# Turning attention weights with the transpose instruction in one decoder step on Trainium2

## What is computed

```
s = q @ k.T * SCALE - slope * dist            # masked
p = softmax(s)
o = p @ v
o = gate[0] * o_cmp + gate[1] * o_sel + gate[2] * o_win
h = x + concat(o, pooled) @ w_out
h = h + peer_ffn(rmsnorm(h))                  # 16 x 16 product keys, 16384 experts
```

## Time and profile before

| what | us |
|---|---|
| median of 3 runs | 1799.54 |
| the 3 runs | 1788.93, 1807.98, 1799.54 |
| the profiled execution | 1798.42 |
| its span in the trace | 1796.8 |

### The profile page before, as it was taken

The page is one execution under the profiler, slowest core; times in us unless marked ns, Lnnn a source line. Parts: engine busy times, 40 slices in busy tenths (PEclk is TensorE's granted clock), DMA queues, the critical chain, the costliest instruction groups (busy, mean ns, idle before and its releaser), DMA issues.

```text
span 1796.8 us, 30054 instructions
## 1 busy us (share of the span) xinstructions
PE 1718.7 (96%) x10604; PEld 1629.2 (91%) x10604; DVE 1359.3 (76%) x2802; ACT 739.5 (41%) x1391; POOL 452.8 (25%) x374
## 2 busy tenths in 40 slices
PE   7997988889999899999999999997999999999999
PEld 6875776668999899999999999996999899999999
DVE  2065334565578899999998998874899899999996
ACT  1022234344321443456666667752333333333332
POOL 0001100001100023323232325442334444444430
PEclk9898988899999999999999999998999999999999
DMA  8314412222322378989899889998799999999994
GB/s 278 86 61 158 119 44 63 80 72 83 106 71 72 114 279 301 327 289 323 317 318 314 311 296 346 381 360 306 289 391 377 361 403 389 386 389 390 390 389 151
DMA packets 196760, 457.33 MB, mean 255 GB/s; under 512 B 25842, under 2 KB 102898, under 8 KB 196146
## 3 DMA queue, kind: packets, MB, share of 16 engines
q1 hardware_dynamic: 123730, 252.93, 40.2%
q0 software_dynamic: 47440, 175.54, 26.5%
q10 hardware_dynamic: 25440, 26.93, 4.4%
HBM read 402.71 MB, written 56.05 MB: 255 GB/s over the span
## 4 chain that ended last, share of the span: by engine, by line
PE 59%; DVE 4%; DMA 2%; issue 1%; ACT 0%; DVEq 0%; SPq 0%; ACTq 0%
PE ps L1896 9%; PE ps L1899 9%; PE ps L1902 9%; PE ps L1872 9%; PE ps L1869 9%; PE ps L1868 9%; PE ps L1918 5%; DMA gates_dense<-sb_g_stage 1%; DVE sb_w_lo L1701 1%; DMA sb_ring<-expert_v 1%; DVE sb_slot L1738 0%; DMA sb_ring<-expert_u 0%; DVE sb_expert_row L1820 0%; DVE sb_rows_y L1831 0%; DVE sb_hot L1737 0%
## 5 line engine op out<-in xcount | busy, mean ns | idle before, releaser
L1609 ACT ACTIVATE sb_w_hi<-sb_ring 128x1024 fp32r<-128x1024 f32 x256 | 272.3, 1064 | 538.1 <-PE ps L1902 270.4
L1701 DVE TENSOR_TENSOR sb_w_lo<-sb_ring,sb_w_hi 128x1024 fp32r<-128x1024 f32 x256 | 313.5, 1225 | 75.4 <-ACT sb_w_hi L1609 71.6
L1868 PE MATMUL ps<-sb_x_hi,sb_w_hi 128*128 128x384 f32 x1024 | 352.5, 344 | 10.6 <-ACT sb_scores L1621 8.0
L1869 PE MATMUL ps<-sb_x_lo,sb_w_hi 128*128 128x384 f32 x1024 | 347.6, 339 | 0.0
L1896 PE MATMUL ps<-sb_x_lo,sb_w_hi 128*128 128x384 f32 x1016 | 200.7, 339 | 9.6 <-ACT sb_x_lo L1616 9.6
L1872 PE MATMUL ps<-sb_x_hi,sb_w_lo 128*128 128x384 f32 x1024 | 202.6, 339 | 4.9 <-DVE sb_w_lo L1701 4.8
L1868 PEld LDWEIGHTS ps<-sb_x_hi,sb_w_hi 128*128 128x128 f32 x1024 | 193.9, 189 | 11.1 <-ACT sb_w_hi L1609 11.1
L1899 PE MATMUL ps<-sb_x_lo,sb_w_lo 128*128 128x384 f32 x1016 | 199.6, 338 | 0.0
L1902 PE MATMUL ps<-sb_x_lo,sb_w_hi 128*128 128x384 f32 x1016 | 198.9, 337 | 0.0
L1869 PEld LDWEIGHTS ps<-sb_x_lo,sb_w_hi 128*128 128x128 f32 x1024 | 194.3, 190 | 0.0
L1896 PEld LDWEIGHTS ps<-sb_x_lo,sb_w_hi 128*128 128x128 f32 x1016 | 180.5, 189 | 11.4 <-issue 8.6
(11 more groups left out here) (326 smaller groups left out, 2560.3 us busy)
## 6 DMA issues: line engine op xcount, KB each, us to landing
sb_ring<-expert_u SPq DMA_DIRECT2D x128, 512.0 KB
sb_ring<-expert_v SPq DMA_DIRECT2D x128, 512.0 KB
gates_dense<-sb_g_stage ACTq DMA_DIRECT2D x12, 2048.0 KB
hid_dense<-sb_hid SPq DMA_DIRECT2D x112, 192.0 KB
sb_scores<-hid_dense SPq DMA_DIRECT2D x112, 192.0 KB
sb_g_stage<-gates_dense SPq DMA_DIRECT2D x32, 384.0 KB
sb_g_stage<-gates_dense SPq DMA_DIRECT2D x48, 256.0 KB
sb_ring<-peer_wq SPq DMA_DIRECT2D x16, 512.0 KB
```

The lines of the kernel that those rows point to most:

```text
L1609: nc.scalar.activation(whi[v % 2][:, :], ring(v)[:, :], ACT.Copy).then_inc(w_hi, 1)
L1701: nc.vector.tensor_tensor(wlo[v % 2][:, :], ring(v)[:, :], whi[v % 2][:, :], ALU.subtract).then_inc(w_lo, 1)
L1868: nc.tensor.matmul(out, hi[:, c * P:(c + 1) * P], g.x_hi[:, c], start=(c == 0), stop=False)
L1869: nc.tensor.matmul(out, hi[:, c * P:(c + 1) * P], g.x_lo[:, c], start=False, stop=False)
```

## The change

The weights are no longer put on a diagonal. VectorE multiplies the exponentials in place in `p[u % 3]` by the row weight, `n` columns for each of the two heads, and TensorE turns the blocks with its transpose instruction, with the identity as the other operand. The diagonal tiles go away, and with them VectorE's wait for `turned`. The four groups of gathered tokens in `output_and_queries` are turned with the transpose instruction too.

```
-        diag = cut(4 * P).rearrange("p (k b n) -> p k b n", k=2, b=2)
...
             def turn(u):
                 j, qt, br = UNITS[u]
-                pe.wait_ge(diags, u + 1)
+                pe.wait_ge(weighed, u + 1)
                 for gg in range(KVH):
                     if u:
                         pe.wait_ge((t_act, t_dve)[gg], u)
                     for kb in range(qt + 1):
-                        last = nc.tensor.matmul(bank(g, 2 + gg)[:, kb * P:(kb + 1) * P], p[u % 3][gg][:, kb * P:(kb + 1) * P], diag[:, u % 2, gg],
-                                                start=True, stop=True)
+                        last = nc.tensor.transpose(bank(g, 2 + gg)[:, kb * P:(kb + 1) * P], p[u % 3][gg][:, kb * P:(kb + 1) * P], g.c["c_ident"][:, :])
                 last.then_inc(turned, 1)
...
                 dve.wait_ge(exps, u + 1)
                 if u >= 2:
-                    dve.wait_ge(diags, u - 1)
+                    dve.wait_ge(weighed, u - 1)
                 link(nc.vector.reciprocal(wt[:, u % 2], rs[:, u % 2]))
                 gate = g.gates[:, qt, 8:24].rearrange("p (b g j) -> p b g j", b=2, g=2)[:, br, :, j]
                 link(nc.vector.tensor_tensor(wt[:, u % 2], wt[:, u % 2], gate, ALU.mult))
-                if u >= 2:
-                    dve.wait_ge(turned, u - 1)
+                n = (qt + 1) * P
                 for gg in range(KVH):
-                    last = nc.vector.tensor_scalar(diag[:, u % 2, gg], g.c["c_ident"][:, :], wt[:, u % 2, gg:gg + 1], None, ALU.mult)
-                last.then_inc(diags, 1)
+                    last = nc.vector.tensor_scalar(p[u % 3][gg][:, 0:n], p[u % 3][gg][:, 0:n], wt[:, u % 2, gg:gg + 1], None, ALU.mult)
+                last.then_inc(weighed, 1)
...
             for k in range(KC):
-                last = nc.tensor.matmul(bank(g, 6 + k // 4)[:, (k % 4) * P:(k % 4 + 1) * P], g.xT[:, k, T - P:T],
-                                        g.c["c_ident"][:, :], start=True, stop=True)
+                last = nc.tensor.transpose(bank(g, 6 + k // 4)[:, (k % 4) * P:(k % 4 + 1) * P], g.xT[:, k, T - P:T], g.c["c_ident"][:, :])
             last.then_inc(rows_mm, 1)
...
```

More of the change, by code:

```diff
@@ L592, in attend @@
         imp, pen, drop = sb("s_imp", [P, NBLK]), sb("s_pen", [P, NBLK]), sb("s_drop", [P, 4])
-        score_mm, score_mm1, score_max, score_max1, biased, exps, diags, turned, t_act, t_dve, o_mm, o_out = map(sem, (
-            "score0_mm", "score1_mm", "score0_max", "score1_max", "biased", "exps", "diags", "turned", "t_act", "t_dve", "o_mm", "o_out"))
+        score_mm, score_mm1, score_max, score_max1, biased, exps, weighed, turned, t_act, t_dve, o_mm, o_out = map(sem, (
+            "score0_mm", "score1_mm", "score0_max", "score1_max", "biased", "exps", "weighed", "turned", "t_act", "t_dve", "o_mm", "o_out"))
         c_mm, c_sub, c_exp, c_wt, c_turn, c_out, chain = map(sem, ("c_mm", "c_sub", "c_exp", "c_wt", "c_turn", "c_out", "chain"))
@@ L1234, in _ @@
                     for k in range(KC):
-                        last = nc.tensor.matmul(bank(g, 6 + k // 4)[:, (k % 4) * P:(k % 4 + 1) * P], x4[:, 0, k].rearrange("p q t -> p (q t)"),
-                                                g.c["c_ident"][:, :], start=True, stop=True)
+                        last = nc.tensor.transpose(bank(g, 6 + k // 4)[:, (k % 4) * P:(k % 4 + 1) * P], x4[:, 0, k].rearrange("p q t -> p (q t)"), g.c["c_ident"][:, :])
                     last.then_inc(rows_mm, 1)
@@ L1241, in _ @@
             for k in range(KC):
-                last = nc.tensor.matmul(bank(g, k // 4)[:, (k % 4) * P:(k % 4 + 1) * P], xn[:, k, T - P:T],
-                                        g.c["c_ident"][:, :], start=True, stop=True)
+                last = nc.tensor.transpose(bank(g, k // 4)[:, (k % 4) * P:(k % 4 + 1) * P], xn[:, k, T - P:T], g.c["c_ident"][:, :])
             last.then_inc(rows_mm, 1)
@@ L1247, in _ @@
             for k in range(KC):
-                last = nc.tensor.matmul(bank(g, 2 + k // 4)[:, (k % 4) * P:(k % 4 + 1) * P], x4[:, 1, k].rearrange("p q t -> p (q t)"),
-                                        g.c["c_ident"][:, :], start=True, stop=True)
+                last = nc.tensor.transpose(bank(g, 2 + k // 4)[:, (k % 4) * P:(k % 4 + 1) * P], x4[:, 1, k].rearrange("p q t -> p (q t)"), g.c["c_ident"][:, :])
             last.then_inc(rows_mm, 1)
```

## The result

The changed kernel's median is 1780.26 us (15 runs, 1774.19 to 1784.27); the old kernel's, measured beside it, 1790.65 us (15 runs, 1782.94 to 1807.98). The ratio is 0.9935, 95% interval [0.9915, 0.9956]: 10.4 us less, where I had forecast 6.2. The absolute time lies 12.7 us under my 1793: 4.2 us is gain that I did not count, and some 9 us is the base, since the three runs of before that I started from have a median 8.9 us above that of all fifteen.

The account below looks back on a forecast made before the run. TensorE bounds attention to 282.5 us, then SyncE's transfer chain runs close behind it. Savings 3.7 + 3.0 + 0.9 - 2.3 + 0.9 = 6.2 us from the 1799.5 median give 1793; range 1784 to 1803.

Parts of the forecast that it names:

- Price of a block: TensorE's turns: a transpose takes 0.109 us, a float32 product 0.222; a block saves 0.113 us at full clock.
- unit 5: Attention before 282.5 us: its six blocks run at half clock and save 0.7 to 1.4 us, taken as 1.0.
- Up to 282.5 us: First attention stretch, bound by TensorE: units 0 to 3, 5 and 7 to 9 save 3.7 us; 4 and 6 nothing.
- From 282.5 to 401.2: Second attention stretch: SyncE's transfer chain lets 3.0 us of at least 9.5 count; 6.5 becomes TensorE's wait for values.
- VectorE's chains: Importance and row weights after 282.5 us: longer scaling puts 1 to 1.5 us on the path, covered by the values wait.
- The clock behind the wait: Behind the second `row_values` wait: TensorE restarts at 1.2 GHz and loses 2.3 us, between 0 and 4.5.
- After it: Behind the second `row_values`: turn(31), 8 blocks in 16 records, saves 0.9 us.
- The output block: Four groups, 32 blocks: only the second group's 8 blocks count, 0.9 us; all would be 3.6.
- SyncE's chain does not bind: Rival, second attention stretch: issues run closer than 1.1 us, all 84 blocks count, 15 us saved, 1784.5; chance 0.12.
- Nothing is left: Rival, attention: low-clock stretches move and the values wait eats the gain, about 1799; 0.20 together with two-record transposes.
- The clock sinks: Rival, slots 16 to 32: transposes do not keep TensorE's clock up, 26 us slower, 1826; chance 0.08.
- VectorE becomes the bound: Rival, in-place scaling: at one column a cycle VectorE pays some 6 us more, 1.5 on chains; chance 0.04.

Follow-up runs that it names:

- off_path_units: In-place scaling everywhere, transposes only in units 4, 6, 11, 13, 18, 26 and 28, products elsewhere and in the output block: 1794.55 us, 1.0019 of the old kernel.
- the half: Old kernel with VectorE scaling in place, TensorE still multiplying, now with the identity; output block as products: 0.9971 of the old kernel.
- split_after: Changed kernel with every second page of selected keys and values issued by GpSimd instead of SyncE: 1777.76 us, 0.9918 of the old kernel.
- split_before: Old kernel with every second page of selected keys and values issued by GpSimd instead of SyncE: 1793.83 us, 0.9999 of the old kernel.
- attend_only: Changed kernel with the output block's four token groups as products again, so attention alone is changed: 1780.82 us, 0.9937 of the old kernel.
- changed_again: The whole changed kernel, run and profiled once more: 1779.73 us, 0.9936 of the old kernel.
- output_only: Old kernel with only the output block's four token groups turned by the transpose instruction: 1796.29 us, 1.0026 of the old kernel.
- transpose_run: Changed kernel with 320 extra transposes in one row ahead of the output block, results unused: 1809.01 us.
- scale_then_product: First run of in-place scaling with identity products kept on TensorE, output block as products, against the old kernel: 1789.2 us.
- before_again: The old kernel, unchanged, profiled again: 1798.22 us.

## Why the prediction was right and where it was wrong

The direction and the mechanism held, the size was off: 10.4 us in place of 6.2, and the time outside the range because the base of three runs lay high as well. The steps that failed are terms of the sum. The 2.3 us that the clock was to cost behind the wait for values did not come (0 measured: the granted clock there is 1.00). The wait itself was sized at 6.5 us and is 2.2, so the stretch from 282.5 us gave 4.3 and not 3.0. The stretch ahead of it gave 4.5 and not 3.7. And the base, 1799.5 us, is 1790.7. Point by point, by the first profile of before against that of the changed kernel, whose expert block starts 10.7 us earlier (582.6 against 593.3):

**Price of a block.** 0.109 to 0.110 for a transpose, 0.222 to 0.225 for a product: right. At half clock, six transposes start 1.47 us before what follows them (228.15 to 229.62), 0.245 each where I had twice 0.109. I had unit 5 at 1.0 us, between 0.7 and 1.4; its turn is 1.4 shorter (230.10 to 232.96 before, 228.15 to 229.62 now).

**Up to 282.5 us, 3.7 forecast, 4.5 measured.** The units called off the path are off it (off_path_units). The place of the 0.8 us more is `compressed`, where the low stretch is 3.4 us long and not 6.8: up to its restart TensorE is 1.2 us earlier (units 0 to 3, forecast 1.4), its own products take 0.7 us less, the turn of unit 5 behind them 1.4, units 7 to 9 give 1.3. The half with products has the short stretch too, and its eighth `sub` is 1.0 to 2.2 us earlier than the old kernel's. I had costed the in-place scaling at nothing here; it goes with a shift of the clock that I cannot derive.

**From 282.5 to 401.2, 3.0 forecast, 4.3 measured.** The mechanism is right: TensorE waits for a transfer of values ahead of the second `row_values`, and without SyncE's chain that wait goes (split_after) while nothing changes in the old kernel (split_before). Two sizes are wrong. SyncE's chain of issues took 112.9 us, not 115 (it was 114.3 in the earlier trace rows). And TensorE waited 2.2 us there, not 6.5: of the 11.8 us of busy time saved, 7.4 came back as idle time, some 5.8 of them ahead of the wait for values, which itself grew by 1.6. I had named VectorE's chains as "some 1 to 1.5 us" that the wait for values would cover. They were 2.9 us in the maxima alone. The mistake is in the reason too: I priced the longer scaling, and what counts is that TensorE comes earlier to chains that did not get shorter. They did fall under that cover: this is why splitting the transfers brings under 2 us and not 6.5.

**The clock behind the wait, 2.3 us lost forecast, 0 measured.** The term that failed most. The wait came out a third as long, and the granted clock behind it was 1.00 from 392.4 to 402.2. By the rows of this case a wait of 2.2 to 3.2 us is followed by a low stretch in one profile and not in another (2.23 us: full, 2.44 us: low, 2.46 us: full, 2.71 us: full, 3.24 us: low), so I had no ground to take it as certain. With this term at nothing my own sum would have been 8.5.

**After it.** turn(31) 0.9: measured 1.0 (2.05 to 1.09). The output block 0.9: measured 0.9 (181.3 to 180.4). Both right. Row values to output: 10.8 us before, 9.8 now.

**Sum.** 4.5 + 4.3 + 1.0 + 0 + 0.9 = 10.7. But the old attention usually ends 3 us later than in the profile that I had (414.8 to 415.3 against 412.0), so against the repeats the trace gives about 14 us at the experts. The differences of the medians are 10.4 in the first pair, 12.5 in attend_only's and 15.2 in changed_again's. The record has the reason for much of this. In 10 of the 31 executions of before beside attend_only the mean granted clock is 0.975 or more, and their median is 1784.4 us; in the other 21 it is 0.967 to 0.974, and 1795.8. No execution of the changed kernel is above 0.972. Against the 21, attend_only is 15.0 us shorter, as the trace has it; against the 10 it is 3.6. The medians move with the share of the two kinds (2 of 12 in output_only and 5 of 12 in the half are of the shorter one). No profile caught one of the shorter kind, so what the old kernel does in them is open. So is the expert block, which differs between profiles of one kernel (1203.5, 1199.8 and 1196.7 us in three of before; 1200.0 and 1199.9 in two of the changed one).

**The rivals.** *SyncE's chain does not bind* (1784.5): refuted as a mechanism, by the wait for a transfer and by the pace of the issues (32 in 34.8 to 35.3 us, in the earlier trace rows 34.5 to 35.8). That the time that it gave is nearest is luck. *Nothing is left* (1799): refuted. *The clock sinks* (1826): refuted for turns between other work, as a loss of that size, by the time itself (the granted clock of the second stretch went from 0.86 to 0.82, and a small part for the transposes in it is not excluded), and for a run of 320 by transpose_run, at a granted clock of 1.00 for 33.8 us. The Trainium skill, "TensorE: Matmul & The Clock Gate", Part 4 (PE-mode transpose), says that the full clock does not engage for transposes, which do not count as busy in the same way; this case's trace does not agree, at 1.00 over that run, and the measurement decides. What transposes do from the low level by themselves, no run here shows: the run began at full clock. *VectorE becomes the bound*: in the form in which I put it, a price of one column a cycle, no (483 ns for 512 columns, by the earlier trace rows about 484). In another form it has come half true: its chains of importance and row weights now end more of TensorE's waits than any transfer.

**The base.** I carried a difference over to a median of three runs that lay 19 us apart, and gave it 3 us of spread, at the upper end alone. It was 8.9 us off. At my own forecast of 6.2 the true base would have given 1784.4, and the measured time would still have been 4 us lower.

## What to carry to other kernels

When an engine's work on the path shrinks by 12 us, do not stop at the first chain that binds next: list the engine's waits by releaser, and ask of each how much it grows when the engine arrives earlier; here the second binding chain (VectorE) lay less than 2 us behind the first (SyncE). A product with an identity or diagonal in float32 costs twice what a transpose does, and scaling in place on an engine that has room pays for it. A difference of two profiles that meets a clock stretch of 7 us is good to 3 us only, so repeat the profile of the kernel before as often as that of the change, and sort the executions by their mean granted clock before comparing medians.

## What the runs showed of the hardware

- Behind the same wait of 2.70 us, with the same instructions around it, the 1.2 GHz level lasted until 2.8 us after the wait's end in one kernel (scale_then_product) and 6.1 us in another (before_again). Twelve records of turning take 1.60 us in the one and 2.93 in the other.
- Executions of the old kernel fall into two kinds by the mean granted clock: 0.975 to 0.980, median 1784.4 us, 10 of 31; 0.967 to 0.974, median 1795.8 us, 21 of 31.
- A float32 transpose of a 128 by 128 block is one record, 0.110 us at 2.4 GHz; 320 in a row with nothing between them kept the granted clock at 1.00 (402.2 to 436.0 us), as products did.
- SyncE's issue of a page whose number it first loads took 1.1 us (32 in 34.5 to 35.8 us); with two engines issuing side by side each kept about its pace, GpSimd one each 1.14 us, SyncE 16 in 17.1 (split_after).
- VectorE scales in place at the price of scaling into another tile: 283, 351, 418 and 483 ns for 128, 256, 384 and 512 columns of float32.
